# A two-layer diffusion step with PEER experts: convolution products placed between attention units, modulation tiles spread over four stages, expert inputs split into latent products and a prompt product

## What is computed

```
mp = modulation(c_ctx, w_mod[l]);  ms = modulation(c, w_mod[l])      # six rows of 1024 each
h = rmsnorm(x, g1) * (1 + scale) + shift
z = h @ w_in;  gb, gc, xa, q, k, v = split(z)                        # layer 0
y_a = gb * short_conv3(gc * xa, conv_w);  y_b = window attention(rope(q), rope(k), v)
x = x + gate * (concat(y_a, y_b) @ w_out)
h = adaln(x);  q = h @ wq;  sc = q . subkeys;  16 best pairs of each of 8 heads -> idx, gsm
act = gelu(h . u_tab[idx]);  x = x + gate2 * sum(gsm * act * v_tab[idx])
```

## Time and profile before

| what | value |
|---|---|
| median of 3 runs | 4620.28 us |
| profiled execution: time, span | 4617.94 us, 4616.1 us |
| PE busy, DVE, ACT, POOL | 96%, 71%, 26%, 42% of the span |
| granted TensorE clock, mean | 0.976 |
| in-projection and attention of layer 0 | 66 to 375 us |
| `u` stage of layer 0, of layer 1 | about 587 to 1606 us, about 2876 to 3895 us |
| value stages | about 1606 to 2310 us, 3895 to 4600 us |

### The profile page before, as it was taken

The page is one execution under the profiler, slowest core; times in us unless marked ns, Lnnn a source line. Parts: engine busy times, 40 slices in busy tenths (PEclk is TensorE's granted clock), DMA queues, the critical chain, the costliest instruction groups (busy, mean ns, idle before and its releaser), DMA issues.

```text
span 4616.1 us, 76065 instructions
## 1 busy us (share of the span) xinstructions
PE 4415.5 (96%) x27516; PEld 4019.7 (87%) x27516; DVE 3265.7 (71%) x6397; ACT 1197.8 (26%) x1696; POOL 1945.9 (42%) x1206
## 2 busy tenths in 40 slices
PE   7878999999999999999988889999999999999998
PEld 6857999999999988888886689999999999888887
DVE  6873199969999597877633432993599995766665
ACT  2043110022332233333233420101232332333332
POOL 2322455644444364444341134555444443544440
PEclk9978999999999999999998999999999999999999
DMA  5401234548777898888520012444477778888884
GB/s 202 161 19 46 67 112 125 181 118 165 161 153 159 218 354 312 312 314 309 204 74 23 24 60 67 119 125 118 117 159 163 158 152 241 321 287 294 288 287 141
DMA packets 823654, 797.70 MB, mean 173 GB/s; under 512 B 566513, under 2 KB 601041, under 8 KB 822898
## 3 DMA queue, kind: packets, MB, share of 16 engines
q1 hardware_dynamic: 175248, 500.38, 32.6%
q10 hardware_dynamic: 603106, 159.70, 16.1%
q0 software_dynamic: 45056, 134.38, 8.3%
HBM read 640.41 MB, written 153.89 MB: 172 GB/s over the span
## 4 chain that ended last, share of the span: by engine, by line
PE 82%; ACTq 8%; DVE 5%; ACT 3%; issue 2%; DMA 0%; DVEq 0%
PE acc L515 14%; PE acc L517 14%; PE acc L516 14%; PE aux L758 5%; PE acc L760 5%; PE acc L758 5%; PE aux L760 5%; PE aux L759 5%; PE acc L759 5%; ACTq L1048 4%; ACTq L1081 4%; PE aux L730 2%; PE aux L573 1%; ACT gates L1098 1%; PE aux L680 1%
## 5 line engine op out<-in xcount | busy, mean ns | idle before, releaser
L515 PE MATMUL acc<-a_hi,w_hi 128*128 128x320 f32 x5296 | 1673.5, 316 | 45.8 <-DVE a_lo L1288 32.9
L517 PE MATMUL acc<-a_hi,w_lo 128*128 128x320 f32 x5296 | 1643.8, 310 | 0.1
L516 PE MATMUL acc<-a_lo,w_hi 128*128 128x320 f32 x5296 | 1643.5, 310 | 0.0
L515 PEld LDWEIGHTS acc<-a_hi,w_hi 128*128 128x128 f32 x5296 | 1000.6, 189 | 50.9 <-issue 34.5
L516 PEld LDWEIGHTS acc<-a_lo,w_hi 128*128 128x128 f32 x5296 | 1000.9, 189 | 1.7 <-issue 0.5
L517 PEld LDWEIGHTS acc<-a_hi,w_lo 128*128 128x128 f32 x5296 | 999.0, 189 | 0.5 <-issue 0.3
L442 POOL TENSOR_TENSOR w_lo<-w_in,w_hi 128x1024 fp32r<-128x1024 f32 (+1 forms) x345 | 902.4, 2616 | 27.6
L458 POOL CAST w_hi<-w_in 128x1024 fp32r<-128x1024 f32 x256 | 311.3, 1216 | 1041.7 <-DMA w_in<-in_u 1041.7
L1526 DVE SCALAR_TENSOR_TENSOR one_b<-iota_b,picks_t 128x384 bf16<-128x384 bf16 x1024 | 632.9, 618 | 0.0
L1524 DVE TENSOR_SCALAR one_a<-iota_b,picks_t 128x128 bf16<-128x128 bf16 x1024 | 573.1, 560 | 60.0 <-PE aux L730 55.0
L467 POOL DMA_INDIRECT found<-in_v,where_i x256 | 315.3, 1231 | 509.1 <-DVE total L1586 401.7
(11 more groups left out here) (246 smaller groups left out, 5423.1 us busy)
## 6 DMA issues: line engine op xcount, KB each, us to landing
w_in<-in_u SPq DMA_DIRECT2D x256, 512.0 KB, 4.0
w_in<-in_v SPq DMA_DIRECT2D x256, 512.0 KB, 4.8
gate_s<-gates ACTq DMA_DIRECT2D x64, 1024.0 KB, 14.0
ag<-act_s SPq DMA_DIRECT2D x256, 256.0 KB, 5.0
ag<-gate_s SPq DMA_DIRECT2D x256, 256.0 KB, 6.1
act_s<-a_out ACTq DMA_DIRECT2D x184, 256.0 KB, 3.7
act_s<-tmp ACTq DMA_DIRECT2D x72, 256.0 KB, 3.6
w_in<-in_in SPq DMA_DIRECT2D x32, 512.0 KB, 4.6
```

The lines of the kernel that those rows point to most:

```text
L515: pe.matmul(out, wh, hi[:, k, n], start=(k == 0), stop=False)
L516: pe.matmul(out, wh, lo[:, k, n], start=False, stop=False)
L517: return pe.matmul(out, wl, hi[:, k, n], start=False, stop=(k == kt - 1))
```

## The change

1. Expert inputs: a chunk's product covers the 512 latent tokens only, in one bank of `acc0` (`latent_steps`: 8 steps of three matmuls of 512 columns). After each four chunks one product makes the prompt tokens of all four, with the tokens as stationary and the four chunks' weights as moving operand (`prompt_steps`: 8 steps of 512 columns, into a bank of `acc1`). `act_p` is now stored once for four chunks, in rows of 2 KB. A slot is free when the prompt product is done (`made_p`), so four loads are issued at once.
2. In the late part the gate groups stand after every fifth step of 40 (`four_chunks`), and chunks 64 to 127 are split by ACT (`high_u`) and DVE (`low_u`) rather than POOL. The bridge is four chunks rather than one, and the end without gates is four rather than seven.
3. Layer 0: two convolution products are made before attention, ten are placed ahead of attention units 0, 3, 6 ... 27 (`conv_beside`), with DVE's three pieces of a convolution after units. The scores use two banks rather than three.
4. Modulation tiles of layer 0: 10 ahead of the rotation, 6 within attention, 8 beside the out-projection, and 8 (rows 40 to 47) before the 16 of layer 1, after `route(0)`. DVE computes the gather indices ahead of these tiles.
5. Slots are counted from the first `u` chunk of each layer.

```
@@ -241,12 +269,15 @@
         FIRST_MOD = 16
         MODS_U = 16
         MODS_AT = range(6 * SPLIT, 7 * SPLIT)
-        MOD_BESIDE = {1: 2, **{n: 3 for n in range(6, 10)}, **{n: 2 for n in range(10, 19)}}
-        MOD_BEFORE_ROPE, MOD_BEFORE_CONV = 14, (6, 4, 4, 4)
+        MODS_LATE = 8
+        MODS_B, MODS_D, MODS_C = range(16, 26), range(26, 32), range(32, 40)
+        B_BESIDE, D_BESIDE = range(1, 6), (8, 9, 11, 12, 14, 16)
+        C_BESIDE = {25: (0, 5), 26: (5, 6), 27: (6, 7), 28: (7, 8)}
+        D_AT = (7, 9, 16, 18, 25, 27)
         EARLY = 7
-        BRIDGE = 1
-        BUILT = 2
+        BRIDGE = GROUP
+        LATE = NKEY // 2
+        SPLIT_BOTH = NKEY - LATE + NKEY
         OUT = {l: product_at(l, "out") for l in range(2)}
         WQ = {l: product_at(l, "wq") for l in range(2)}
...
-        A_EARLY = EARLY * SPLIT // 2
-        A_LATE = (NKEY - EARLY * SPLIT) // 4
+        A_EARLY = (EARLY * SPLIT + BRIDGE) // 2
+        A_LATE = (NKEY - EARLY * SPLIT - BRIDGE) // 4
...
-        MIXED_AT = [3, 5, 7, 9] + [2 * NT * (j + 1) + 4 for j in range(3)]
+        CONV_FIRST, CONV_EVERY = 2, 3
+        MIXED_AT = [31, 32, 33, 34, 35, 36, 37]
...
-            return (aux[0][:, 0, :], aux[0][:, 1, :], acc[0][:, 0, :])[u % 3]
+            return aux[0][:, u % 2, :]
+        def conv_beside(v):
+            c = CONV_FIRST + v // CONV_EVERY
+            return c if v >= 0 and v % CONV_EVERY == 0 and c < 12 else None
...
-                                    sp.wait_ge(mod_used, k - 1 - (FIRST_MOD - BY_DVE))
+                        if l == 0 and n in B_BESIDE:
+                            for k in MODS_B[2 * (n - 1):2 * n]:
+                                if n > 1:
+                                    sp.wait_ge(mod_used, used(k - 2))
                                 sp.dma_start(w_mod_b[:, k % 2], a["w_mod"][0, k]).then_inc(mod_b_in[k % 2], 16)
-                            tile += MOD_BESIDE.get(n, 0)
-                def load_inputs(c, u):
-                    slot = (UC[l] + u) % SPLIT
-                    sp.wait_ge(made, UM[l] - SPLIT + 1 + c)
...
-            for m in range(IN[0] + 6, IN[0] + 18):
+            for m in range(IN[0] + 6, IN[0] + 6 + CONV_FIRST):
                 by_feature(m)
...
             for v in range(NUNIT):
+                if conv_beside(v) is not None:
+                    by_feature(IN[0] + 6 + conv_beside(v))
+                if v == 0:
+                    scores_of(2)
                 if v + 3 < NUNIT:
...
+                def latent_steps(m0, w, taken_value, split, split_value):
+                    pe.wait_ge(split, split_value)
                     pe.wait_ge(taken[m0 % 2], taken_value)
-                    spots = [2 * KD * (j + 1) // beside - 1 for j in range(beside)]
-                    for h in range(2):
-                        n = slice(h * HALF, (h + 1) * HALF)
-                        for k in range(KD):
-                            mm = linear_step(acc[m0 % 2][:, h, 0:HALF], w, P, k, KD, a_hi, a_lo, n)
-                            if h == 1 and k == KD - 1:
-                                mm.then_inc(made, 1)
-                            if KD * h + k in spots:
-                                between()
-                with pe.Fori(0, EARLY) as i:
-                    for u in range(SPLIT):
-                        expert(UM[l] + u, (UC[l] + u) % SPLIT, split_by_pool(UC[l] + u) + SPLIT * i,
-                               (UM[l] + u) // 2 + (SPLIT // 2) * i)
-                for c in range(SPLIT * EARLY, SPLIT * EARLY + BRIDGE):
-                    expert(UM[l] + c, (UC[l] + c) % SPLIT, split_by_pool(UC[l] + c), (UM[l] + c) // 2)
+                    for k in range(KD):
+                        mm = linear_step(acc[0][:, m0 % 2, :], w, P, k, KD, a_hi, a_lo, slice(P, T))
+                        if k == KD - 1:
+                            mm.then_inc(made, 1)
+                        yield
+                def prompt_steps(g, first_slot, bank):
+                    if l or not (isinstance(g, int) and g < 2):
+                        pe.wait_ge(taken_p, FOURS * l + g - 1)
+                    w, n = slice(first_slot, first_slot + GROUP), slice(0, P)
+                    for k in range(KD):
+                        wh, wl = w_hi[:, w, k * P:(k + 1) * P], w_lo[:, w, k * P:(k + 1) * P]
+                        pe.matmul(acc[1][:, bank, :], a_hi[:, k, n], wh, start=(k == 0), stop=False)
+                        pe.matmul(acc[1][:, bank, :], a_lo[:, k, n], wh, start=False, stop=False)
+                        mm = pe.matmul(acc[1][:, bank, :], a_hi[:, k, n], wl, start=False, stop=(k == KD - 1))
+                        if k == KD - 1:
+                            mm.then_inc(made_p, 1)
+                        yield
+                def four_chunks(c, i, far, split, split_value, between=None):
+                    done = 0
+                    for j in range(GROUP + 1):
+                        if j < GROUP:
+                            m0 = UM[l] + c + j
+                            steps = latent_steps(m0, (c + j) % SPLIT, m0 // 2 + far // 2 * i, split,
+                                                 split_value(c + j) + far * i)
+                        else:
+                            steps = prompt_steps(c // GROUP + far // GROUP * i, c % SPLIT, c // GROUP % 2)
+                        for _ in steps:
+                            done += 1
+                            if between is not None and done % 5 == 0:
+                                between(done // 5 - 1)
...
+                def late(i, first=False):
+                    for g in range(GROUP):
+                        c = EARLY * SPLIT + BRIDGE + GROUP * g
+                        def next_four(q):
+                            gates_of_four(GROUPS * l + 8 * g + q + 32 * i, 8 * g + q)
+                        if first and g == 0:
+                            four_chunks(c, 0, 0, lo_done, by_pool, next_four)
+                        else:
+                            four_chunks(c, i, 4 * GROUP, lo_v, by_both, next_four)
...
+                def prompt(g, k):
+                    act.wait_ge(made_p, FOURS * l + g + 1)
+                    if not (isinstance(g, int) and g < 2 and l == 0):
+                        act.wait_ge(p_st[k], 16 * (FOURS // 2) * l + 8 * (g - k))
+                    act.activation(p_out[k][:], acc[1][:, k, :], ACT.Gelu_apprx_tanh).then_inc(taken_p, 1)
+                    act.wait_ge(taken_p, FOURS * l + g + 1)
+                    act.dma_start(act_p_rows[l][:, bass.ds(4 * P * g, 4 * P)], p_out[k][:]).then_inc(p_st[k], 16)
...
+                def high_u(c, i):
+                    act.wait_ge(raw_in[c % SPLIT], 16 * LOADS[UC[l] + c] + 32 * i)
+                    act.activation(w_hi[:, c % SPLIT, :], landing(c % SPLIT), ACT.Copy).then_inc(hi_v, 1)
...
+                        take_gates(i, g, 0)
+                        take_chunk(0)
+                        take_gates(i, g, 1)
+                        take_gates(i, g, 2)
+                        take_chunk(1)
+                        take_gates(i, g, 3)
+                        high_u(first + GROUP, i)
+                        take_chunk(2)
+                        take_gates(i, g, 4)
+                        high_u(first + GROUP + 1, i)
+                        take_gates(i, g, 5)
+                        high_u(first + GROUP + 2, i)
+                        take_chunk(3)
+                        high_u(first + GROUP + 3, i)
+                        take_gates(i, g, 6)
+                        prompt(first // GROUP + 4 * i, first // GROUP % 2)
+                        take_gates(i, g, 7)
                 late(0)
...
+                for after, piece in enumerate((conv_in, conv_sum, conv_out)):
+                    c = conv_beside(u - 3 - after)
+                    if c is not None and c % 3 == 2:
+                        piece(c // 3)
+                if u in D_AT:
+                    i = D_AT.index(u)
+                    modulate_next(MODS_D[i], w_mod_d[i % 2][:], mod_d_in[i % 2], i // 2 + 1)
...
+                        for j in ((), (0,), (1,), (2, 3))[max(0, q % 8 - 4)]:
+                            low_u(LATE + GROUP * (q // 8) + j, i)
+                def low_u(c, i):
+                    dve.wait_ge(hi_v, input_by_both(l, c) + 4 * GROUP * i)
+                    dve.tensor_tensor(w_lo[:, c % SPLIT, :], landing(c % SPLIT), w_hi[:, c % SPLIT, :].bitcast(F),
+                                      ALU.subtract).then_inc(lo_v, 1)
```

More of the change, by code:

```diff
@@ L49, with slots @@
 CHUNKS, PRODUCTS = plan()
+def slots():
+    slot, before, loads, had = [], [], [], {}
+    start = {l: next(n for n, c in enumerate(CHUNKS) if c[:2] == (l, "u")) for l in range(2)}
+    for n, chunk in enumerate(CHUNKS):
+        w = (n - start[chunk[0]]) % SPLIT
+        last, count = had.get(w, (None, 0))
+        slot.append(w)
+        before.append(last)
+        loads.append(count + 1)
+        had[w] = n, count + 1
+    return slot, before, loads
```

(2 more changed lines are left out.)

326 lines of the change are left out of this document (191 added, 135 removed).

## The result

Four runs of the changed kernel took 4675.93 to 4682.55 us, median 4679.95, against 4621.48 for the kernel before: ratio 1.0131, 95% interval 1.0111 to 1.0151. It is 58 us slower where 60 us faster was forecast, and above the forecast's range. The profiled execution has a span of 4674.1 us, 58.0 above the 4616.1 of before.

The account below looks back on a forecast made before the run. PE was taken to bound the early part, ACT's held gate stores the late part. Front -39, tile loads +3, both layers' experts -24 sum to -60 us: 4560 us as a median, range 4490 to 4640.

Parts of the forecast that it names:

- Front: Layer 0 up to the first matmul of the out-projection: near 336 us where it was 374.97, so -39 us.
- The two `u` stages: Expert input stages of both layers: -24 us from new products and late pace, +3 for layer 0's modulation tiles.
- the tile loads: Layer 0's early part: SP's modulation tile loads delay chunk loads; +3 us, within 0 to 11.
- Rival A: Late part: four loads at once hold gate stores back fully; D 19.3, period 37.7, total about 4643 us; chance 0.18.
- The loop: Late part: ACT, held by gate stores, sets the pace; X = D + 18.4 = 35.1 us per four chunks.
- D: Late part: time from gate store issue until the `act_s` store behind is issued; put at 16.7 us.
- D's own part: Late part: what the 2 MB of gate stores take of D without the loads; 13.7 us.
- the loads' part: Late part: transfer work of four loads issued together that overlaps the gate stores; 3.0 us of D.
- the rest of the loop: Late part, beyond D: 2.6 to PE's bank, 13.1 of PE's steps, 2.7 of ACT's work; 18.4 us.
- break-even of 35.9: Late part: period of four chunks at which the `u` stage would neither gain nor lose; 35.9 us.
- I take 15.5: Layer 0's attention: a cycle of three units and one convolution product takes 15.5 us, the product partly hidden.
- Rival C: Layer 0's attention: products not hidden, DVE's pieces delay softmax, clock stays 0.71; front +6, total 4605 us; chance 0.15.

Follow-up runs that it names:

- experiment 2: Changed kernel, but SP issues the four loads of the late part only once the gate stores of the same four chunks have landed: 4589.08 us, ratio 0.9942.
- experiment 5: Changed kernel with only the first half of each chunk loaded and split in chunks 64 to 127, the rest left out: one run, 4618.74 us.
- experiment 3: Changed kernel with all twelve convolution products and DVE's convolution pieces ahead of attention, six tiles staying within it: 4670.14 us, ratio 1.0110.
- experiment 4: Changed kernel with each of the ten products beside attention cut into three pieces, placed behind the scores of the unit three ahead: 4628.47 us, ratio 1.0020.
- experiment 6: Changed kernel with layer 0's early tile loads eight at a time behind chunks 51, 55, 59, route's buffer wait behind chunk 51's load: 4676.29 us.
- experiment 1: Changed kernel with the gate stores issued by SP, behind the loads of the same four chunks, instead of ACT: 4578.88 us, ratio 0.9913.
- experiment 9: Changed kernel with chunks 64 to 127 split by POOL again, none by ACT and DVE, gate stores staying with ACT: 4810.53 us, ratio 1.0414.
- experiment 10: Changed kernel with chunks 64 to 127 split by POOL again and the gate stores issued by SP: 4814.66 us, ratio 1.0421.
- experiment 8: Kernel before the change with its gate stores issued by SP, a store behind every fourth load: 4694.73 us, ratio 1.0159.

## Why the prediction was wrong

**Where the error of 118 us lies.** Front: +21.9 us against a forecast of -39, 61 off. The two `u` stages: +29.6 against -21 (-24 and +3 for the tile loads), 51 off. Between the `u` stages: +6.4 against nothing. (Rival A's own 4643 lay above the stated range, though the range was said to take all but A's far end.)

**The late part's mechanism was right, its size wrong.** The loop, its members and its reading (ACT's issues first, PE's 33.2 behind) held. The terms: D's own part put at 13.7, measured 14.85; the loads' part put at 3.0, measured 3.35; the rest of the loop 18.4, measured 18.65. Together 36.85 rather than 35.1. The largest of the three misses, 1.15 us, is D's own part: 2 x 2^20 bytes at 145 GB/s are 14.5 us, which the prediction rounded to 14 and then took as 13.7. The period before was read from nine fours as 35.2, and is 34.97 over both layers. So where the sum had 0.1 us less in each of the fours, there are 1.9 more. That holds for the 15 intervals between gate stores, 28 us a layer; the sixteenth four, ahead of the first stores, has no stall and came out 4.0 us shorter in layer 1, which the sum did not have. Layer 1's `u` stage in parts, forecast and measured: early part +7.3, +3.4; the sixteen fours -1.6, +24.2; the end -18, -17.8. The period lies two thirds of the way from the forecast to rival A's 37.7, just under the 37.0 from which A was to decide; D did not reach A's 19.3. A's direction is that of the rule it was set beside, that each DMA engine serves the queues in turn, a packet at a time (the Trainium skill, DMA: Bandwidth & Descriptors, "Queues, rings and completion order"). Experiments 2 and 5 agree with the direction, 3.35 us of D for four loads and 1.15 for four halves; how the packets share an engine no run here shows. With a forecast of 35.1 and a break-even of 35.9, an error of 0.8 us in the loop was enough to turn the sign of this stage, and the members were not known that well.

**Attention was wrong in its step.** "I take 15.5" for a cycle of three units and one product lay between the sum's 12.5 for a product wholly hidden and 19.5 to 20 for none; measured 20.3, which is 43 of the 61 us. Two errors. The unit was taken as 2.46 us from two late units, where the mean over all 40, from DVE's first read of scores to its last, is 3.1:

```profile
245.20 0.29 DVE L1413 TENSOR_SCALAR s_sb<-aux 128x128 f32<-128x128 f32 x1
```

(366.86 - 245.20)/39 = 3.12, so 2 us of each cycle and 26 over the 40 units. And nothing of a product hid, since the scores stand behind it in PE's queue, and it took 8.3 us rather than 7.0: experiment 3 shows its full time, experiment 4 takes 52 us out with the same products in other places. The rest of the 61: the rotation ended at 145.1 rather than 135, so the third product began 8.5 us late, and 55.9 us follow the start of the last product rather than 46. Rival C had the product ahead of the scores right, but not the delay by DVE's pieces nor a clock that stays at 0.71; its +6 was built on the same short unit, and does not follow from its own 19.5 to 20 a cycle either, which give -3 to +2. It was +21.9. The rise of the clock, from which I argued for hiding, came in part (0.71 to 0.82, not above 0.9) and bought nothing: both engines wait in turns. The two score banks, put at nothing, were not tested by themselves: in experiment 3 a unit without its tiles took 3.27 us against 3.12, with two banks and a clock of 0.63 rather than 0.71, so the two together cost some 8 us there.

**Tile loads in the early part:** forecast +3, within 0 to 11; measured 6.05 us of waits and some 8 in all (experiment 6). The wait for route's buffers ahead of chunk 48's load, which holds all of these loads, was not in the sum; experiment 6 moved it together with the tile loads, so which of the two cost the time is open.

**Not in the sum:** 6.4 us between the `u` stages, of which 3.96 is one wait at the start of layer 0's values, behind the modulation tile that lands late after four value loads. Slots freed by fours make that burst as well. The prediction put the value stages at nothing since they read the same bytes. The other 2.4 us are not traced.

**Right:** four early chunks take 27.19 us (27.17). So a matmul's fixed part is here the 12.8 ns of the rows. The Trainium skill's about 2.5 ns (TensorE: Matmul & The Clock Gate, "Wait - 56ns, not 53.3ns?") does not fit this trace. Also right: moving strided weights costs nothing; PE's own late period, 33.6 in experiment 1 against 33.2; eight tiles beside the out-projection and the eight behind `route(0)` are hidden on DVE; DVE does not hold up PE in the changed kernel. That last was right for a reason that the prediction did not have: POOL does nothing in that stretch any more. The end without gates, four chunks rather than seven, gave 17 us back, as forecast (18).

**Open:** the kernel before lost 75 us with its stores on SP. Shown are that PE waits for DVE there, that POOL's splits slow DVE's operations as much with either engine's stores, and that with SP's stores the splits come in bursts. That the bursts alone make PE wait fits experiments 9 and 10, where they are longer and the loss is larger, but no run spread the splits out again.

## What to carry to other kernels

An engine that issued 2 MB in short runs was held for 7.5 to 12 of the 13 to 17 us until they landed; let one that has nothing due issue them (here 101 us for moving two calls). In the kernel before, where SP had loads due behind the stores, the same move lost 75 us: look at what stands behind them in the new queue as well. When work is put between the steps of a latency loop, what counts is what stands behind it in the same queue: place it after the instructions that the other engine needs next, and in pieces not longer than the wait. Price a loop by its mean over the stage, not by its best pair, and when loads are freed in groups, ask what each group will hit all at once.

## What the runs showed of the hardware

Beside POOL's subtraction of 128 x 1024 (2.5 us) DVE's 128 x 128 operation takes 2.4 us rather than 0.24, and its 128 x 384 operation at times 1.4 rather than 0.60 (experiment 9). A pair of gate stores of 1 MB each took 7.5 to 7.7 us to issue with none to two loads beside them (the kernel before, experiments 2 and 8), and 10 to 12 with four loads of 512 KB under way, from ACT (the changed kernel) and from SP (experiment 1) alike.
